# Normed activations and the shared region moved 320 bytes up in SBUF, against split weights that stay

## The reference

```python
def _swiglu(h, w_in, w_out):
    gate, up = jnp.split(h @ w_in, 2, axis=-1)
    return (jax.nn.silu(gate) * up) @ w_out
...
for li in range(DEPTH):
    g = norm_gains[li]
    x = x + 0.5 * _swiglu(_rmsnorm(x, g[0]), ffn_w_in[li, 0], ffn_w_out[li, 0])
    h = _rmsnorm(x, g[1])
    x = x + (_hgrn2_mixer(h, ...) if li < N_A_LAYERS else _mla_mixer(h, ...))
    x = x + 0.5 * _swiglu(_rmsnorm(x, g[2]), ffn_w_in[li, 1], ffn_w_out[li, 1])
    gate = jax.nn.sigmoid((_rmsnorm(x, g[3]) @ ple_w_gate[li]).astype(jnp.float32))
    x = x + (gate * (p[li] @ ple_w_in[li]).astype(jnp.float32)).astype(x.dtype)
```

## The kernel before, in words

| tensors | bytes | modulo 512 |
|---|---|---|
| `w_raw`, `w_hi`, `w_lo` | 16512, 32896, 65664 | 128 |
| `X`, `sq`, `ones`, `const` | 98432, 106624, 116864, 117376 | 128 |
| `ckh`, `ckl`, `krz` | 128704, 130752, 132800 | 192 |
| `xh`, `xl` | 139840, 148032 | 64 |
| `region` with `hh`, `hl`, `oh`, `ol`, `hg_*`, `cqh`, `cql`, `pth`, `ptl`, `mod_raw`, `mod_acc`, `gate_t` and others | from 156224 | mostly 64 |

## Time and profile before

### The profile page before, as it was taken

The page is one execution under the profiler, slowest core; times in us unless marked ns, Lnnn a source line. Parts: engine busy times, 40 slices in busy tenths (PEclk is TensorE's granted clock), DMA queues, the critical chain, the costliest instruction groups (busy, mean ns, idle before and its releaser), DMA issues.

```text
span 1612.6 us, 31237 instructions
## 1 busy us (share of the span) xinstructions
PE 1528.2 (95%) x12299; PEld 1468.0 (91%) x12299; DVE 1107.4 (69%) x1659; ACT 779.7 (48%) x1259; POOL 184.7 (11%) x224
## 2 busy tenths in 40 slices
PE   7999998989999989999999999999997999989998
PEld 6999998989999989999989799999997976889767
DVE  5886559965886577875676746975588458394583
ACT  5554374454543456443453635543464338253481
POOL 1111015501111010111010001111023000020000
PEclk9999999999999999999999999999998999999999
DMA  7787644425776645776645154876644613075010
GB/s 223 239 264 241 219 131 131 124 75 162 234 251 215 219 130 174 248 224 197 205 121 151 52 165 153 273 235 194 209 149 140 172 41 105 1 228 174 21 53 26
DMA packets 219308, 264.85 MB, mean 164 GB/s; under 512 B 22253, under 2 KB 197325, under 8 KB 219213
## 3 DMA queue, kind: packets, MB, share of 16 engines
q1 hardware_dynamic: 209136, 234.58, 46.6%
q0 software_dynamic: 8960, 27.37, 5.2%
q10 hardware_dynamic: 1117, 1.57, 0.3%
HBM read 262.44 MB, written 1.05 MB: 163 GB/s over the span
## 4 chain that ended last, share of the span: by engine, by line
PE 70%; DVE 15%; ACT 6%; DMA 6%; issue 3%; POOL 0%; DVEq 0%; SPq 0%; ACTq 0%
PE bank L1006 20%; PE bank L1008 20%; PE bank L1007 20%; DVE w_lo L1674 6%; DMA mod_raw<-in_w_ada 3%; PE bank L1574 2%; ACT w_hi L646 1%; DMA w_raw<-in_ffn_w_in 1%; PE bank L1413 1%; PE bank L1607 1%; DVE rs L1686 1%; ACT xh L657 1%; DVE hg_s L1902 1%; ACT sq L664 1%; DVE mod_acc L1706 1%
## 5 line engine op out<-in xcount | busy, mean ns | idle before, releaser
L1006 PE MATMUL bank<-xh,w_lo 128*128 128x256 f32 x2312 | 653.3, 283 | 25.3 <-DVE xl L2157 13.5
L646 ACT ACTIVATE w_hi<-w_raw 128x1024 fp32r<-128x1024 f32 x452 | 454.4, 1040 | 438.8 <-PE bank L1008 279.0
L1674 DVE TENSOR_TENSOR w_lo<-w_raw,w_hi 128x1024 fp32r<-128x1024 f32 x452 | 547.9, 1248 | 153.7 <-ACT w_hi L646 152.5
L1007 PE MATMUL bank<-xl,w_hi 128*128 128x256 f32 x2312 | 648.5, 280 | 0.0
L1008 PE MATMUL bank<-xh,w_hi 128*128 128x256 f32 x2312 | 648.3, 280 | 0.0
L1006 PEld LDWEIGHTS bank<-xh,w_lo 128*128 128x128 f32 x2312 | 439.6, 190 | 30.2 <-DVE xl L2157 14.5
L1007 PEld LDWEIGHTS bank<-xl,w_hi 128*128 128x128 f32 x2312 | 439.4, 190 | 1.1 <-issue 0.7
L1008 PEld LDWEIGHTS bank<-xh,w_hi 128*128 128x128 f32 x2312 | 437.5, 189 | 0.2
L1006 PE MATMUL bank<-hh,w_lo 128*128 (+1 forms) x704 | 197.3, 280 | 5.8 <-DVE w_lo L1674 5.8
L1007 PE MATMUL bank<-hl,w_hi 128*128 (+1 forms) x704 | 196.4, 279 | 0.0
L1008 PE MATMUL bank<-hh,w_hi 128*128 (+1 forms) x704 | 196.4, 279 | 0.0
(11 more groups left out here) (365 smaller groups left out, 2185.1 us busy)
## 6 DMA issues: line engine op xcount, KB each, us to landing
w_raw<-in_ffn_w_in SPq DMA_DIRECT2D x176, 512.0 KB, 4.7
w_raw<-in_ffn_w_out SPq DMA_DIRECT2D x88, 512.0 KB, 4.4
w_raw<-in_w_in SPq DMA_DIRECT2D x52, 512.0 KB, 4.7
mod_raw<-in_w_ada POOLq DMA_DIRECT2D x128, 192.0 KB, 4.3
w_raw<-in_a_w_in SPq DMA_DIRECT2D x32, 512.0 KB, 4.5
w_raw<-in_ple_w_gate SPq DMA_DIRECT2D x16, 512.0 KB, 4.3
w_raw<-in_b_w_out SPq DMA_DIRECT2D x16, 512.0 KB, 4.2
w_raw<-in_w_out SPq DMA_DIRECT2D x16, 512.0 KB, 3.6
```

What stands on the lines that cost most here:

```text
L646: A(w_hi[:, c % NSLOT, cols], w_raw[:, c % NRAW, cols], ACT.Copy).then_inc(*did(hi_ready))
L1006: mm(out, lhs[1], rhs[0], start=start, stop=False, skip_group_check=skip)
L1007: mm(out, lhs[0], rhs[1], start=False, stop=False, skip_group_check=skip)
L1674: V.tensor_tensor(w_lo[:, c % NSLOT, cols], w_raw[:, c % NRAW, cols], f32(w_hi[:, c % NSLOT, cols]), ALU.subtract).then_inc(*did(lo_ready))
```

## The change

One line is added in front of `xh`. It leaves 320 bytes unused, so that `xh`, `xl` and everything from `region` up move by 320 bytes; what lies below stays. No instruction is added, removed or moved on any engine; only SBUF addresses change. `xh` then starts at 140160 and `region` at 156544, both at 384 modulo 512, against 128 for the split weights: 256 bytes apart instead of 64. `ckh` and `ckl` stay at 192. 320 is a multiple of 64, so offsets modulo 64 stay as they were.

```diff
@@ -198,6 +198,7 @@
     gpre = fixed("gpre", [P, KD])
     gpost = fixed("gpost", [P, KD])
     ptok = fixed("ptok", [P, 2, TB, T])
+    base[0] += 320
     xh = fixed("xh", [P, KD, T], F32R)
     xl = fixed("xl", [P, KD, T], F32R)
     region = base[0]
```

## The result

The changed kernel takes 1649.79 us (median of 4, 1647.45 to 1651.71) against 1610.61 us for the kernel before (median of 4, 1601.73 to 1617.17). The ratio is 1.0238, with a 95% interval of 1.0196 to 1.028: slower by 2.4%, 39.2 us. The forecast was 1607, with a range up to 1634. The profiled execution of the changed kernel took 1647.45 us, 33.0 more than the profiled one of before.

A forecast was written before the change was run, and what follows sets the result against it. TensorE's rate of matmul starts was taken to bound the kernel. The only term, the rate's dependence on operand distance, was put at zero, so the forecast was the median, 1607 us, with a range from 1586 to 1634.

The forecast's parts named there:

- What bounds the kernel: Whole kernel: TensorE's matmul rate limits the long stages, busy 1528.2 of 1612.6 us; the rest is handing over between stages.
- the zero for all other users of the moved memory: Gate, up and hidden tiles, `mod_raw` and its DMA, attention tiles: costed at nothing, since offsets modulo 64 stay.
- Two rates, settled at the start of a stream: Split matmul streams: 113.3 or 117.8 ns per start, settled by timing at each stream's start, varying between executions.
- I take zero for the term, for three reasons: Split matmul streams: the operands' relative place changes the rate by nothing, 0 us.
- The first reason: Two feed-forward windows: both rates, 113.3 and 117.8 ns, occur at the same distance, so the address alone doesn't choose.
- The second reason: Streams in `tokens` and the latent, moving tile 64 bytes above: 117.4 and 111 ns, again the two rates.
- The third: Reason: a slow `tokens` stream ran at DMA 0.00, a quick stretch at DMA share 0.95; other engines' traffic isn't the cause.
- The bounds: All split matmuls: none slow 1591.8 us, all slow 1639.1, at weight-load rate 1539, against the profiled 1614.45.
- The third rival: Stream starts behind waits: more streams run slow at the new distance, 4.45 ns a matmul, 1639 us if all; chance 0.28.
- What would show it: Feed-forward windows after: both 113.3 and 117.8 ns confirm the forecast; one rate alone, below 112, or another rate refutes it.
- the 24-column chunk: Stream with weight tiles stepping by 96 bytes: went from 117.5 to 114 ns without a wait, speaking for an address effect.
- a rival in which the distance matters: Split matmul streams: at 256 bytes apart the tiles don't meet, all run at 113.3 ns, 1592 us; chance 0.20.

The follow-up runs named there:

- all320: 320 bytes put in front of w_raw against the kernel before, so every tensor moves and no distance changes; 1605.21 us in one execution.
- up256: The change's line with 256 bytes in place of 320, against the kernel before; 1623.58 us in one execution.
- up64: The change's line with 64 bytes in place of 320, so activations and weights start at distance 0, against the kernel before; 1647.6 us, ratio 1.0217.
- lo128: Only w_lo moved by 128 bytes against the kernel before, all else keeping its offset modulo 512; 1598.67 us, ratio 0.9915.
- the sweep: Kernels with the change's line at other shifts, 32 to 480 bytes in place of 320, against the kernel before; rates compared by distance, times between 1610.61 and 1649.79 us.
- up384: The change's line with 384 bytes in place of 320, activations 64 above the weights modulo 256, against the kernel before; 1629.77 us in one execution.
- lo_meets: Only w_lo moved by 192 bytes, to distance 0 modulo 256 from the activations, against the kernel before; 1637.07 us in one execution.
- hi_meets: Only w_hi moved by 192 bytes, to distance 0 modulo 256 from the activations, against the kernel before; 1634.31 us in one execution.
- up512: The change's line with 512 bytes in place of 320, distance modulo 512 as before, against the kernel before; 1612.07 us, ratio 1.0002.
- weights192: Split weights moved by 192 bytes instead of the activations, distance to the activations 256, against the kernel before; 1646.04 us in one execution.

## Why the prediction was wrong

**What bounds the kernel** was right. TensorE's rate of starts is what the time follows, and no other engine's busy time changed by more than 1 us, so the zero for all other users of the moved memory held. Two readings were loose: the windows of rows 3 lie in two feed-forwards, not in one loop, and the quick window is the one whose matmuls last 276 ns, the slow one 281.

**Two rates, settled at the start of a stream** was right as far as it went: all320 and up256 differ from the kernel before in which loops are quick, at the same distance. That the choice varies between executions of one kernel is not shown, since each was traced once. I had put the spread of the timed executions down to it, and the runs support only part of that. At a distance with one rate the spread is small (after: 4.3 us over 4; up64: 5.6 over 4), but lo128, whose windows are all quick, still spreads over 10.5 us in 9.

**The step that failed** is "I take zero for the term, for three reasons". The term, the dependence of the rate on the distance of the two operands, measured 39.2 us of TensorE's busy time: quick streams went from 113.3 to 120.0 ns, slow ones from 117.8 to 120.0. The first reason, that both rates occur at one distance, shows that the address alone doesn't choose between them; I read it as if the address didn't matter, and the sweep says that the distance sets which rates there are to choose from. The second reason used the only other distance that full tiles have in the trace, 64 above in place of 64 below. By chance these are two places with the same two rates (up384 has them too), so the agreement said little about the places in between; two points don't show that a function is flat. The third, that other engines' traffic isn't the cause, was right, and should have made me ask what else is left.

**The bounds** failed with it. I built them from the rates that the trace showed, and so took 117.8 ns for the worst. The rate at this distance is 120.0 ns in every long stream that moved. The third rival came nearest: it had the distance as the cause, and the sign, though that the crossing of the tiles is what acts wasn't shown, and its price of 4.45 ns a matmul was too small. Against the profiled execution, 5,530 matmuls lost 6.7 ns and 5,100 lost 2.2, 48 us together. Of the signs in "What would show it" two came true, the third rival's (a value of 117.8 or larger alone) and the last (a rate other than the two, at granted clock 1.00).

**The evidence for an effect**, the 24-column chunk, pointed at the address for a reason that doesn't hold. Its third tile, at weight offset 320, is at distance 0 modulo 256 from `xh`, and there its three starts took 0.34 us (from 1297.11), 113 ns each, the quick rate. The rows of its last start in the first layer, of its first and last in the second layer, and of its first and last in the first layer of the changed kernel:

```profile
1299.04 0.28 PE L1008 MATMUL bank<-xh,w_hi 128*24 128x256 f32 x1
```

```profile
1493.47 0.28 PE L1006 MATMUL bank<-xh,w_lo 128*24 128x256 f32 x1
...
1496.17 0.28 PE L1008 MATMUL bank<-xh,w_hi 128*24 128x256 f32 x1
```

```profile
1322.36 0.28 PE L1007 MATMUL bank<-xh,w_lo 128*24 128x256 f32 x1
...
1324.99 0.28 PE L1009 MATMUL bank<-xh,w_hi 128*24 128x256 f32 x1
```

Its 23 intervals take 2.63 us in the first layer (from 1296.41) and 2.70 in the second, and 2.63 after the change. So the chunk differs between the layers at the same addresses, and it is the one moved stream of split matmuls that I found not slowed by the change. What was measured for full tiles doesn't carry over to it. That it led to a rival in which the distance matters was luck.

**Where the rest went.** 48 us by count and 33 measured between the profiles. 6 us of it is idle time that got shorter: TensorE was idle 84.4 us of its span before and 78.2 after. Most of that is the wait for the split weights. The waits view (us in total, times, longest), before and after:

```profile
PE bank L1006 <- DVE w_lo L1674: 9.1, 6, 3.4
```

```profile
PE bank L1007 <- DVE w_lo L1675: 3.7, 4, 2.0
```

With slower matmuls ScalarE and VectorE have the next slot ready in time more often: 5.4 us less. Busy time grew by 39.2 us, 9 less than the count gives. The starts in the two traces tell where these are. Between split matmuls that start within 150 ns of each other the mean interval rose from 115.4 ns (10,321 intervals) to 119.9 (10,364), 46 us and so nearly the count's 48. The longer intervals between split matmuls, around waits and restarts, shrank from 76.2 us (264 of them) to 61.3 (221), and all intervals with other matmuls from 335.6 us to 331.8.

**Why the distance counts** stays open. The Trainium skill, in its page SBUF — State Buffer, section "Who interferes with whom", says that TensorE never waits on anyone and has a port for each of its two reads. The measured rates, 113.3 against 120.0 ns by nothing but the distance of the two operands, don't go with the reading of it that the prediction used, that an offset changes nothing, and here the measurement decides. That the two reads of TensorE disturb each other in SBUF is a possible explanation, but it was argued, not shown: lo_meets and hi_meets were to show it, and didn't.

## What to carry to other kernels

Where a kernel is bound by a long stream of equal matmuls, divide a window by its count and look for more than one rate at full clock; if there is more than one, the start addresses of the moving and the stationary tiles are worth a sweep in steps of 32 bytes over 256, each operand by itself, since shifts of 32 to 320 bytes that touch no instruction moved this kernel between -0.85% (lo128) and +2.4% (the change). One trace at each place isn't enough where a place has several rates; the times of several executions tell which place is better. A layout change made for other reasons can move these addresses too, and then two versions differ for a reason that no diff of instructions shows. And a forecast of no effect needs more than two points at which there was none.

## What the runs showed of the hardware

The rates of float32r matmuls with 128 x 128 stationary and 128 x 256 moving tiles depend on the distance of the two in SBUF, as far as tested with a period of 256 bytes. In the windows of this case a distance of 0 gave 120.0 ns from start to start, 64 below 113.3 or 117.8, 32 below 118.2, 32 above 116.5 to 117.7, and 128 gave 118.6. Several distances have more than one rate; at 64 below each of the two held for over 100 us of a loop, and what chooses between them isn't known. A set of rates stays the same when all addresses move (all320), and the DMA share doesn't set the rate: it was 0.76 in a window at 113.2 ns (up512) and 0.79 in one at 120.0 (weights192). The shortest mean interval of these matmuls in the windows above was 113 ns. With a 24-column stationary tile the rule for full tiles did not hold (2.63 us for 23 intervals before and after the change).
